# Mean squares of the new residual as wide products in four column groups with a fold, and row spreads as transposes

## What is computed

```python
mix = jnp.concatenate([y_ret, y_ssm], axis=-1) @ w_out[i]
x = x + rmsnorm(mix, norm_mix_post[i])
h = rmsnorm(x, norm_mlp_pre[i])
m = jnp.square(jax.nn.relu(h @ w_ff1[i])) @ w_ff2[i]
x = x + rmsnorm(m, norm_mlp_post[i])
```

## Time and profile before

| | us |
|---|---|
| median of 3 runs | 2968.2 |
| lowest and highest | 2966.32, 2975.13 |
| the profiled execution's own time | 2962.38 |
| its span | 2960.6 |
| mean granted TensorE clock | 0.967 |

### The profile page before, as it was taken

The page is one execution under the profiler, slowest core; times in us unless marked ns, Lnnn a source line. Parts: engine busy times, 40 slices in busy tenths (PEclk is TensorE's granted clock), DMA queues, the critical chain, the costliest instruction groups (busy, mean ns, idle before and its releaser), DMA issues. The chain is left out here.

```text
span 2960.6 us, 33695 instructions
## 1 busy us (share of the span) xinstructions
PE 2794.9 (94%) x13054; PEld 2272.4 (77%) x13054; DVE 1687.3 (57%) x2244; ACT 613.5 (21%) x990; POOL 978.0 (33%) x515
## 2 busy tenths in 40 slices
PE   7899999999999999969998998889999999999997
PEld 6788878878888888857785775568777888888885
DVE  8787535746655666765658956754176322222247
ACT  3223232210111000232321006532122100011111
POOL 2122215553333333521122330002454433333353
PEclk9999999999999999978999998999999999999998
DMA  3111132223232323221011332140232211111122
GB/s 133 37 51 47 57 128 86 85 84 102 93 92 85 97 88 106 86 93 39 29 36 64 122 108 83 70 164 29 72 113 87 64 50 50 50 43 50 50 71 100
DMA packets 88346, 228.83 MB, mean 77 GB/s; under 512 B 27504, under 2 KB 30576, under 8 KB 88240
## 3 DMA queue, kind: packets, MB, share of 16 engines
q1 hardware_dynamic: 52240, 172.67, 18.1%
q10 hardware_dynamic: 36000, 54.69, 6.0%
HBM read 197.84 MB, written 28.31 MB: 76 GB/s over the span
## 5 line engine op out<-in xcount | busy, mean ns | idle before, releaser
L194 POOL CAST w_hi<-w_raw 128x1024 fp32r<-128x1024 f32 x254 | 285.6, 1124 | 1921.4 <-PE ps L207 1910.2
L203 PE MATMUL ps<-a_hi,w_hi 128*128 128x512 f32 x2080 | 691.5, 401 | 45.0 <-PEq L2770 18.9
L196 POOL TENSOR_TENSOR w_lo<-w_raw,w_hi 128x1024 fp32r<-128x1024 f32 x254 | 689.5, 2714 | 20.3
L205 PE MATMUL ps<-a_lo,w_hi 128*128 128x512 f32 x2080 | 676.0, 393 | 0.0
L207 PE MATMUL ps<-a_hi,w_lo 128*128 128x512 f32 x2080 | 674.9, 393 | 0.0
L203 PEld LDWEIGHTS ps<-a_hi,w_hi 128*128 128x128 f32 x2080 | 390.9, 191 | 133.0 <-issue 30.3
L207 PEld LDWEIGHTS ps<-a_hi,w_lo 128*128 128x128 f32 x2080 | 394.7, 190 | 85.0
L205 PEld LDWEIGHTS ps<-a_lo,w_hi 128*128 128x128 f32 x2080 | 395.5, 190 | 83.6
L205 PE MATMUL ps<-g_b,w_hi 128*128 128x512 f32 x1216 | 418.3, 395 | 0.0
L203 PE MATMUL ps<-g_b,w_hi 128*128 128x512 f32 x1088 | 370.2, 398 | 6.3 <-DVE g_b L1733 6.3
L207 PE MATMUL ps<-g_b,w_lo 128*128 128x512 f32 x1088 | 366.7, 394 | 0.0
(11 more groups left out here) (424 smaller groups left out, 3023.8 us busy)
## 6 DMA issues: line engine op xcount, KB each, us to landing
w_raw<-in_wstream SPq DMA_DIRECT2D x254, 512.0 KB, 3.5
ada_w<-in_ada_w ACTq DMA_DIRECT2D x25, 512.0 KB, 3.5
ada_w_m<-in_ada_w ACTq DMA_DIRECT2D x25, 512.0 KB, 3.5
y_by_token<-y ACTq DMA_DIRECT2D x12, 512.0 KB, 3.1
x_res_b<-in_xT SPq DMA_DIRECT2D x2, 2048.0 KB, 11.6
x_block<-x_res_b SPq DMA_DIRECT2D x16, 256.0 KB, 3.3
z_rows<-ada_w ACTq DMA_DIRECT2D x8, 512.0 KB, 2.7
u_rows<-pad ACTq DMA_DIRECT2D x8, 512.0 KB, 4.6
```

The lines of the kernel that those rows point to most:

```text
L194: pool.tensor_copy(k.w_hi[:, s, :], k.w_raw[:, s, :]).then_inc(k.w_high, 1)
L196: pool.tensor_tensor(k.w_lo[:, s, :], k.w_raw[:, s, :], k.w_hi[:, s, :].bitcast(F32), ALU.subtract).then_inc(k.w_split, 1)
L203: pe.matmul(o, w_hi, a_hi[:, c], start=first, stop=False)
L205: pe.matmul(o, w_hi, a_lo[:, c], start=False, stop=False)
```

## The change

The new sums of `sums_new_pe` are turned round. For each tile `t` there is one fp32 product: `mean_col`, broadcast to 32 columns, is the loaded operand, the 512 squares of the half move, and the result has 32 equal rows. Tile `t` writes to the rows of column group `t % 4`, so two tiles add up in each group, and the four groups stand in one PSUM bank of 128 rows. ACT copies this bank to `w.acc` (`parts_act`), and `fold_new_pe` sums over the 128 rows with `fold_col` = 4/128 in 4 products of one column. In `output_halves_pe` all eight wide products now stand in the middle of tile 4, the fold behind tile 4, and the row in the middle of tile 5. In `half_step` the two parts of four keep their places, the fold stands in the middle of the second second-layer tile, and the row keeps its place. The second half of turn 2 keeps the old form (`tail_sums_pe`). Apart from this, all spreads become `pe.transpose` of the broadcast column.

```diff
@@ -360,8 +361,8 @@
             for c in range(NC):
-                ins = pe.matmul(Xf[1][:, c * P:(c + 1) * P], rcol[:, c:c + 1].broadcast_to([P, P]), ident,
-                                start=True, stop=True)
+                ins = pe.transpose(Xf[1][:, c * P:(c + 1) * P], rcol[:, c:c + 1].broadcast_to([P, P]),
+                                   ident)
...
@@ -693,6 +694,7 @@
             ch.link(dve.memset(k.head_col[:, :], 1.0 / HEAD_DIM))
+            ch.link(dve.memset(k.fold_col[:, :], GROUPS_PE / P))
...
+GROUPS_PE = 4
...
@@ -1060,8 +1065,8 @@
         for c in range(HC):
             at = h * HC + c
-            ins = pe.matmul(k.ps[:, 6 + h, c * P:(c + 1) * P], w.rcol[:, at:at + 1].broadcast_to([P, P]),
-                            k.mats[:, IDENT, :], start=True, stop=True)
+            ins = pe.transpose(k.ps[:, 6 + h, c * P:(c + 1) * P], w.rcol[:, at:at + 1].broadcast_to([P, P]),
+                               k.mats[:, IDENT, :])
         return ins
...
@@ -1071,13 +1076,30 @@
     def sums_new_pe(self, pe, h, ts):
         k, w = self.k, self.w
         for t in ts:
+            g = t % GROUPS_PE
+            pe.wait_ge(self.sq_new, h * KT + t + 1)
+            ins = pe.matmul(k.ps[32 * g:32 * (g + 1), 4 + h, :], k.mean_col[:, :].broadcast_to([P, 32]),
+                            w.mix[:, t, half_of(h)], start=t < GROUPS_PE, stop=t >= KT - GROUPS_PE)
+        if KT - 1 in ts:
+            ins.then_inc(self.parted, 1)
+
+    def fold_new_pe(self, pe, h):
+        k, w = self.k, self.w
+        pe.wait_ge(self.part_out, h + 1)
+        for c in range(HC):
+            at = (h * HC + c) * P
+            ins = pe.matmul(k.ps[:, 4 + h, c:c + 1], w.acc[:, at:at + P], k.fold_col[:, :], start=True, stop=True)
+        ins.then_inc(self.summed, 1)
+
+    def tail_sums_pe(self, pe, h):
+        k, w = self.k, self.w
+        for t in range(KT):
             pe.wait_ge(self.sq_new, h * KT + t + 1)
             for c in range(HC):
                 at = (h * HC + c) * P
                 ins = pe.matmul(k.ps[:, 4 + h, c:c + 1], w.mix[:, t, at:at + P], k.mean_col[:, :],
                                 start=t == 0 and c == 0, stop=t == KT - 1, skip_group_check=True)
-        if KT - 1 in ts:
-            ins.then_inc(self.summed, 1)
+        ins.then_inc(self.summed, 1)
...
+    def parts_act(self, act, h):
+        k, w = self.k, self.w
+        act.wait_ge(self.parted, h + 1)
+        act.activation(w.acc[:, half_of(h)], k.ps[:, 4 + h, :], ACT.Copy).then_inc(self.part_out, 1)
...
@@ -1231,15 +1258,15 @@
             half_tile(h, m, 0)
             if h and m == 1:
                 turn.row_pe(pe, 0)
-            if h and m == 3:
-                turn.sums_new_pe(pe, 0, range(KT // 2))
             if h and m == 4:
-                turn.sums_new_pe(pe, 0, range(KT // 2, KT))
+                turn.sums_new_pe(pe, 0, range(KT))
+            if h and m == 5:
+                turn.row_new_pe(pe, 0)
             half_tile(h, m, 1)
             if h and m == 0:
                 turn.sums_pe(pe, 0)
             if h and m == 4:
-                turn.row_new_pe(pe, 0)
+                turn.fold_new_pe(pe, 0)
@@ -1258,6 +1285,7 @@
     for t in range(6, KT):
         turn.square_new_act(act, t, 0)
+    turn.parts_act(act, 0)
     turn.root_new_act(act, 0)
     take(4, 1)
...
@@ -1521,8 +1549,10 @@
-        def second_layer(t, q, banks, ready):
+        def second_layer(t, q, banks, ready, between=None):
             for half, kt in FIRST_ORDER if t == 0 else NEXT_ORDER:
+                if between and half and kt == 0:
+                    between()
...
@@ -1564,8 +1594,9 @@
-                second_layer(t, q, ([(k.ps[:, 2 * q + h, :], cols)], [(X[q][:, h, :], cols)]), g0)\
-                    .then_inc(k.tile_done, 1)
+                follows = other and other.following and t == 1
+                second_layer(t, q, ([(k.ps[:, 2 * q + h, :], cols)], [(X[q][:, h, :], cols)]), g0,
+                             (lambda: other.fold_new_pe(pe, 1 - h)) if follows else None).then_inc(k.tile_done, 1)
...
@@ -1594,7 +1625,7 @@
         if turn.following:
-            turn.sums_new_pe(pe, 1, range(KT))
+            turn.tail_sums_pe(pe, 1)
             turn.row_new_pe(pe, 1)
...
@@ -1665,6 +1696,7 @@
             if other and other.following:
+                other.parts_act(act, o)
                 other.root_new_act(act, o)
```

More of the change, by code:

```diff
@@ L160, in open_kit @@
     k.mean_col, k.head_col, k.eps = sb("mean_col", [P, 1]), sb("head_col", [P, 1]), sb("eps", [P, 1])
+    k.fold_col = sb("fold_col", [P, 1])
     k.c_silu = sb("c_silu", [P, KT, 2])
@@ L420, in spread @@
                 for c in range(NC):
-                    ins = pe.matmul(Xf[region(p, RSTD)][:, c * P:(c + 1) * P], rcol[:, c:c + 1].broadcast_to([P, P]), ident,
-                                    start=True, stop=True)
+                    ins = pe.transpose(Xf[region(p, RSTD)][:, c * P:(c + 1) * P], rcol[:, c:c + 1].broadcast_to([P, P]),
+                                   ident)
                 ins.then_inc(k.aux_done, 1)
@@ L1043, in __init__ @@
         s = signals(nc, ctx, name, "sq added sums root inv row scaled x_new sq_new summed root_new inv_new row_new "
-                                   "raw hi lo")
+                                   "raw hi lo parted part_out")
         self.sq, self.added, self.sums, self.root, self.inv, self.row = (
@@ L1049, in __init__ @@
         self.raw, self.hi, self.lo = (s[n] for n in ("raw", "hi", "lo"))
+        self.parted, self.part_out = s["parted"], s["part_out"]
     def sums_pe(self, pe, h):
@@ L1348, in spread @@
             for c in range(NC):
-                ins = pe.matmul(Xf[1][:, c * P:(c + 1) * P], rcol[:, c:c + 1].broadcast_to([P, P]), k.mats[:, IDENT, :],
-                                start=True, stop=True)
+                ins = pe.transpose(Xf[1][:, c * P:(c + 1) * P], rcol[:, c:c + 1].broadcast_to([P, P]),
+                                  k.mats[:, IDENT, :])
             ins.then_inc(s["row"], 1)
@@ L1972, in _ @@
             for c in range(CC):
-                ins = pe.matmul(row[:, c * P:(c + 1) * P], rcol[:, c:c + 1].broadcast_to([P, P]), ident,
-                                start=True, stop=True)
+                ins = pe.transpose(row[:, c * P:(c + 1) * P], rcol[:, c:c + 1].broadcast_to([P, P]),
+                                   ident)
             ins.then_inc(s["row"], 1)
@@ L2633, in spread @@
                 at = g * NC + c
-                ins = pe.matmul(Xf[g][:, c * P:(c + 1) * P], w.rcol[:, at:at + 1].broadcast_to([P, P]), ident,
-                                start=True, stop=True)
+                ins = pe.transpose(Xf[g][:, c * P:(c + 1) * P], w.rcol[:, at:at + 1].broadcast_to([P, P]),
+                                   ident)
             ins.then_inc(s["row"], 1)
```

## The result

The kernel with the change takes 2942.07 us (median of 4 runs, 2938.74 to 2943.0), the kernel before beside it 2971.47 us (4 runs). The ratio is 0.990, with a 95% interval of 0.988 to 0.992. The forecast was 2942. The profiled execution has an own time of 2942.41 us and a span of 2940.6 us (before: 2960.6), so 20.0 us went, where the sum of the prediction had 26.4.

What follows compares the result with a forecast made beforehand. TensorE, busy for 94% of the span, was taken as the bound. Terms 2.0 + 4.3 + 4.7 + 1.8 + 4.1 + 4.2 + 5.3 gave 26.4 us off 2960.6; ratio 0.991 on the median gave 2942 us, range 2926 to 2961.

Steps and rivals of the forecast that it cites:

- Turn 1's second half: First block shorter, VectorE's chain ending last, then dense work and fold at full clock: 4.3 us gained.
- turn 2: VectorE's chain 2.5 us earlier, second group 1.4 us shorter, a half-clock stretch gone, fold added: 4.7 us gained.
- turn 3's first half: TensorE waits for late squares of tiles 6 and 7; split 5.7 us earlier, less one half-clock stretch: 4.1 us gained.
- Rivals B: Wide products do not overlap at 32 columns, clock up: eight take 6.9 us, +9.6 us, 2952 us; chance 0.10.
- C: Clock falls behind the wide blocks as behind the narrow ones: +7.2 us, 2949 us; chance 0.09.
- D: Slower: clock stays at half through block, fold and dense work up to the new row: 2980 us; chance 0.04.
- Rival E: Clock falls behind a run of transposes: one 1.6 us stretch behind L2634's 16, 2944 us; chance 0.07.
- starts in order: Wide products: a second record waits for its first while the next product starts beside it; eight take 3.9 us.
- the two readings: Wide products: in-order overlap, 3.9 us for eight, or the skill's up to 4x, the 1.7 us end.
- rival A: Wide products: four groups run together, 6.0 us more gained in all, 2936 us; chance 0.08.
- Turn 1's first half: TensorE 6.3 us earlier, VectorE only 3.7; new wait of 2.6 us and half clock of 1.7: net 2.0 us gained.
- Turn 3's second half: 2.1 us earlier at the second group, 1.4 for the group, 1.6 for a stretch, less 0.9: 4.2 us gained.

Runs made afterwards that it cites:

- the buffers in place: Changed kernel with head_col and fold_col as two columns of one tensor, so g_b stays at byte 100544: 2928.78 us, ratio 0.9875 to the kernel before.
- the swapped groups: Changed kernel with tile t writing to column group t // 2, so neighbouring products share a group: ratio 0.9924 to the kernel before.
- the tile alone: Kernel before with only one unused column of 32 bytes per partition added, no instruction changed: 2978.7 us, ratio 1.0049.
- the run with one group: Changed kernel with all wide products in one group of 128 rows instead of four of 32: ratio 0.996 to the kernel before.
- transposes alone: Kernel before with only the spreads turned into transposes, sums and row as before: ratio 0.9963, 11 us.

## Why the prediction was right, and where it was not

**What held.** TensorE stays the bound. The stretches of half clock behind the blocks went with the blocks. The fold costs 0.8 us to the next dense start and its copy is hidden. A spread is four records. Turn 1's second half (-3.9 for a forecast of -4.3), turn 2 (-3.8 for -4.7) and turn 3's first half (-4.5 for -4.1) came near their terms. In turn 3's first half the wait for the last squares is there, but small: the block of eight takes 2.84 us in place of 1.85 (2164.91 to 2167.75). The larger stop, which the prediction did not name, stands in the half tile ahead of it, for VectorE's `take` (2.5 us), with half clock behind it. Rivals B, C and D fell: the block is short, and the clock behind it is 1.00. Rival E, a fall behind L2634's 16 transposes, did not come either: 1.1 us less there, and 1.9 with the buffers in place, against 1.8 forecast.

**The wide products: 1.85 us, not 3.9.** The step "starts in order" is wrong, as the swapped groups show. The prediction said that L488 can't tell the two readings apart. Its total can't, but its starts can. The timeline of the kernel before, cut off at 173.90 us:
```profile
173.85 0.33 PE L488 MATMUL ps<-u_grp,hT 128*64 128x128 f32 x2
```
Two records start together, 7 ns apart, at the very start of the run, and all 32 records start in 16 such pairs, up to the last. With starts in order the first record would stand alone, since behind it in the stream comes the second record of its own product, which must wait. So the rows of before already spoke for rival A, and its 0.08 was too little. What it cost the sum lies mostly in turn 1's first half.

**Turn 1's first half: -7.2, not -2.0.** The forecast let VectorE's chain eat most of TensorE's gain: a wait of 2.6 us more and a half-clock stretch of 1.7 us behind it. Measured is a wait of 0.44 us on TensorE, and full clock after it:
```profile
537.15 1.05 PE L1061 MATMUL ps<-mean_col,acc_b 128*128 128x1 f32 x8 [0.44 <-DVE acc_b L1153]
```
Two reasons. The shorter block let the chain start at 517.04 and not at 519.1 (2.1 us). And from its start to the sums the chain itself took 20.1 us, where before it took 22.1 (522.81 to 544.90). Most of that is the first add, which before ran beside GpSimd's 2.4 us subtraction (L196, from 523.13) and now stands between two of GpSimd's steps:
```profile
523.13 2.40 POOL L196 TENSOR_TENSOR w_lo<-w_raw,w_hi 128x1024 fp32r<-128x1024 f32 x1
523.48 2.61 DVE L1126 TENSOR_TENSOR acc_b<-acc_b,tmp_b 128x512 f32<-128x512 f32 x1
```
It took 2.61 us there, and 0.69 us in the kernel after. All adds of this form in the trace of before bear it out: the 28 of 56 that meet no such subtraction take 0.68 or 0.69 us, and the 19 that lie inside one for over 2 us take 2.61 to 2.88 us. No run moved GpSimd alone.

**Turn 3's second half: -6.7, not -4.2.** The prediction took 2.1 us off up to the second group, 1.4 for the group and 1.6 for the stretch at 2255.1. Of the three stretches in this part before (3.4 us at 2217.5, 6.8 at 2238.0, 3.4 at 2255.1) one of 3.4 us stayed, at 2218.7, where the prediction had let more stay behind the wait for the squares; and the second block of four took 1.4 us for 2.1. (Where nothing holds it, as at 552.34 and 1244.49, such a block takes 1.0 us.)

**What was missed: the memory.** The prediction gave a cost to each instruction of the diff and not the one tile that it declares. That tile moves the work buffers by 32 bytes and makes the MLPs 11.3 us slower; with the buffers in place the change gives 37.3 us of span (2960.6 to 2923.3), with them moved 20.0. In the profiled execution +11.3 stands against 5.2 in turn 1 and 2.5 in turn 3 that were too small; the other terms came 2.8 us short together, most of it at the start (where L421's 2.7 us came, but also a half-clock stretch of 6.8 us at 286.8 that the execution of before doesn't have) and in turn 2. That makes the difference between 26.4 and 20.0. The time was right because errors of both signs met.

**What stays open.** Why these three places differ. Whether transposes make some of the stretches in phase 1: they stand at 286.8 and 385.8 in one execution of the kernel after, 203.5 and 384.4 in another. Stretches stand there without transposes too, at 385.5 in one execution of the kernel before and at 292.9 and 388.4 in the kernel before with the tile alone, so they come and go. And when exactly a stop is followed by half clock: in two kernels of the same order here, a stop of 2.15 and one of 2.13 us at the same wide product were followed by clock 1.00 in the first and 0.51 in the second, and in two executions of the kernel after a stop of 2.4 us at the same product (562.9) was followed by half clock in one and by 1.00 in the other. So 1.6 us of such a place is chance.

## What to carry to other kernels

Put small reductions over partitions into wide products with 32 equal rows per group: eight fp32 products of 512 columns cost 1.85 us in four groups and a fold of 0.8 us, where 32 products with a one-column moving operand cost 7 us and brought TensorE to half clock behind them. When a diff declares memory, even one element, compare the pace of products that it doesn't touch, and put small constants into a tile that is already there; here 32 bytes cost 11.3 us in the two MLPs, of the 37 us of span that the change could bring. When a total comes out right, compare it stretch by stretch before believing the terms.

## What the runs showed of the hardware

- Column groups of 32 run side by side for fp32 products, four starts 7 ns apart and the second records 0.43 us later. The order of the products over the groups does not matter (1.85 and 1.88 us): a record that waits in its group does not hold those of other groups.
- The start-to-start pace of the same fp32 dense product depends on where in the partition its moving operand lies: 0.2289, 0.2334 and 0.2325 us for places 32 bytes apart, 0.2275 us for another buffer. It does so with all other compute engines idle, and with no DMA packet beside it, too.
- The granted clock stayed at 1.00 behind the wide blocks where TensorE had not stopped beside them, those of 1.9 us in four groups and all of the run with one group (6.5 and 3.0 us). At 38 of the 40 blocks of one-column products in four traces (before twice, transposes alone, the tile alone) it fell to 0.50, though the profile shows TensorE as busy in both.
- A VectorE fp32 add of 128x512 took 0.69 us where no GpSimd subtraction of 128x1024 met it, and 2.6 to 2.9 us where it lay inside one for over 2 us.
- An fp32 transpose of 128 columns is one record and starts 0.11 us before the next; the same as a product with the identity is two. The Trainium skill (TensorE: Matmul & The Clock Gate, Part 4: PE-mode transpose) says that transposes do not count as work for the clock; behind 16 of them in a row no run here showed a fall.
